# Thirty-two experts on one core: the turns of the gated rows and of the next rows move into the middle of the weight products

## The reference, cut to what matters

```
a = xb @ w_gate[e]                       # 1024 x 512
b = xb @ w_up[e]                         # 1024 x 512
y = (silu(a) * b) @ w_down[e]            # 512 x 1024
```

## Time and profile before

| | us |
|---|---|
| median of 3 runs | 2085.39 (2083.49 to 2088.24) |
| the profiled execution, its own time | 2085.79 |
| its span in the profile | 2084.0 |
| TensorE busy | 1966.2 (94% of the span) |
| VectorE busy | 1188.4 (57%) |
| ScalarE busy | 970.2 (47%) |
| 32 experts, from the first GM to the last | 292.2 to 877.9 in the span |

### The profile page before, as it was taken

One profiled execution on the slowest core, in us unless ns is written; L12 is line 12 of the kernel. 1 busy time (PEld: TensorE's weight loads), 2 busy tenths in 40 slices (PEclk: granted clock), 3 DMA queues, 4 the chain that ended last, 5 costly groups with the idle time before them and its releaser, 6 DMA issues.

```text
span 2084.0 us, 22887 instructions
## 1 busy us (share of the span) xinstructions
PE 1966.2 (94%) x8924; PEld 1572.5 (75%) x8924; DVE 1188.4 (57%) x1547; ACT 970.2 (47%) x1469; POOL 186.4 (9%) x250
## 2 busy tenths in 40 slices
PE   4989989999999999989999999998999989999997
PEld 3758767777777777758888888886777768888886
DVE  7776688888888888862543333324345343333322
ACT  3433268778878787744232222124445442222221
POOL 3100110121211110010000000001011100000000
PEclk8999999999999999999999999999999999999999
DMA  8464479999999999952323323222112123323211
GB/s 282 158 210 168 172 245 337 352 352 368 357 351 349 345 335 349 331 174 81 101 81 101 102 81 101 91 91 84 61 41 81 41 68 125 101 98 101 87 39 41
DMA packets 199832, 366.49 MB, mean 176 GB/s; under 512 B 13450, under 2 KB 83863, under 8 KB 199722
## 3 DMA queue, kind: packets, MB, share of 16 engines
q1 hardware_dynamic: 180960, 342.91, 47.6%
q10 hardware_dynamic: 8714, 11.46, 1.6%
q0 software_dynamic: 10048, 10.62, 1.5%
HBM read 365.05 MB, written 24.65 MB: 187 GB/s over the span
## 4 chain that ended last, share of the span: by engine, by line
PE 87%; DVE 7%; DMA 2%; issue 2%; ACT 1%; SPq 1%; POOL 0%; DVEq 0%; POOLq 0%; ACTq 0%
PE ps L263 85%; DVE wlo L210 2%; DMA raw<-in_w_in 1%; PE ps L2031 1%; DVE GM L2104 1%; SPq L886 1%; PE ps L731 1%; DMA raw<-in_ada_w 0%; DMA raw<-in_w_expert_down 0%; DVE acc L260 0%; PE ps L2608 0%; DVE hT5l L260 0%; DVE hT4l L769 0%; DVE X L845 0%; ACT XN L689 0%
## 5 line engine op out<-in xcount | busy, mean ns | idle before, releaser
L210 DVE TENSOR_TENSOR wlo<-raw,whi 128x1024 fp32r<-128x1024 f32 (+1 forms) x576 | 671.5, 1216 | 317.2 <-ACT whi L191 313.7
L191 ACT ACTIVATE whi<-raw 128x1024 fp32r<-128x1024 f32 (+1 forms) x576 | 573.0, 1047 | 232.8 <-PE ps L263 215.2
L263 PE MATMUL ps<-hT5h,whi 128*128 128x512 f32 x352 | 137.8, 391 | 6.3 <-DVE wlo L210 6.3
L263 PE MATMUL ps<-hT5l,whi 128*128 128x512 f32 x352 | 137.5, 391 | 0.0
L263 PE MATMUL ps<-hT3h,whi 128*128 128x512 f32 x352 | 137.0, 389 | 0.6 <-DVE hT3l L260 0.6
L263 PE MATMUL ps<-hT5h,wlo 128*128 128x512 f32 x352 | 137.4, 390 | 0.0
L263 PE MATMUL ps<-hT3l,whi 128*128 128x512 f32 x352 | 136.9, 389 | 0.0
L263 PE MATMUL ps<-hT3h,wlo 128*128 128x512 f32 x352 | 136.9, 389 | 0.0
L2471 DVE TENSOR_TENSOR tmpT<-tmpT,ps 128x512 f32<-128x512 f32 x44 | 30.1, 684 | 139.6 <-PE ps L263 139.6
L263 PE MATMUL ps<-whi,XT1h 128*128 128x512 f32 x256 | 102.1, 399 | 0.0
L263 PE MATMUL ps<-whi,XT0h 128*128 128x512 f32 x256 | 101.0, 395 | 1.1 <-DVE XT0l L2057 1.1
(11 more groups left out here) (446 smaller groups left out, 4062.5 us busy)
## 6 DMA issues: line engine op xcount, KB each, us to landing
raw<-in_w_expert_gate SPq DMA_DIRECT2D x64, 1024.0 KB, 8.2
raw<-in_w_expert_up SPq DMA_DIRECT2D x64, 1024.0 KB, 8.0
raw<-in_w_expert_down SPq DMA_DIRECT2D x64, 1024.0 KB, 6.7
raw<-in_ffn_w_gu SPq DMA_DIRECT2D x44, 1024.0 KB, 5.0
raw<-in_ffn_w_down SPq DMA_DIRECT2D x20, 1024.0 KB, 5.0
raw<-in_ada_w SPq DMA_DIRECT2D x24, 512.0 KB, 5.4
raw<-in_w_in SPq DMA_DIRECT2D x8, 1024.0 KB, 5.7
raw<-in_a_w_in SPq DMA_DIRECT2D x8, 1024.0 KB, 9.3
```

The source lines that it names most:

```text
L191: e.activation(hi[:, c], raw[:, c], ACT.Copy).then_inc(self.S("w_hi"), 1)
L210: e.tensor_tensor(lo[:, c], raw[:, c], hi[:, c].bitcast(F32), ALU.subtract).then_inc(self.S("w_lo"), 1)
L263: return e.matmul(o, l, r, start=start, stop=stop, skip_group_check=True)
```

## The change

The arithmetic is the same. Only the order on three engines and the plan of banks change. The product routine gets a call between its two halves (12 matmuls each). In it `eg` of n runs the 4 transposes of the gated rows of n-1, and `eu` of n runs the 8 transposes of the rows of n+1. ScalarE's and VectorE's loops put the copies of these between the items of the two halves, so that the items that belong to a product's first and second half are taken one at a time (`take_act(e, name, i)`). The last expert's gated rows are turned after its `eu`, as before.

```
@@ the plan of banks
         for n in range(NE):
+            if n > 0:
+                R.plan(f"et{n - 1}", 1, V_)
             R.plan(f"eg{n}", 1, A_)
...
+            if n + 1 < NE:
+                R.plan(f"x{n + 1}", 2, V_)
             R.plan(f"eu{n}", 1, V_)
...
-            if n + 1 < NE:
-                R.plan(f"x{n + 1}", 2, V_)
-            R.plan(f"et{n}", 1, V_)
+        R.plan(f"et{NE - 1}", 1, V_)
         R.plan(f"ey{NE - 1}", 2, A_)
@@ TensorE
-        def rows_in_pe(e, n, name):
+        def rows_in_pe(e, n, name, between=None):
...
                 if q == 0:
                     i.then_inc(S("w_used"), 1)
+                    if between is not None:
+                        between()
...
+        def turn_gated_pe(e, n):
+            b = R.claim(e, f"et{n}")
+            if n == NE - 1:
+                idle_pe(e, b, 2)
+            e.wait_ge(*R.done(f"eu{n}"))
+            for k in range(4):
+                i = e.transpose(b[:, k * P:(k + 1) * P], GM[:, k * P:(k + 1) * P], ident[:, :])
+            i.then_inc(*R.fill(f"et{n}"))
...
             for n in range(NE):
-                rows_in_pe(e, n, "eg")
+                rows_in_pe(e, n, "eg", (lambda: turn_gated_pe(e, n - 1)) if n > 0 else None)
                 if n > 0:
                     rows_out_pe(e, n - 1)
-                rows_in_pe(e, n, "eu")
-                if n + 1 < NE:
-                    turn_pe(e, n + 1)
-                b = R.claim(e, f"et{n}")
-                if n == NE - 1:
-                    idle_pe(e, b, 2)
-                e.wait_ge(*R.done(f"eu{n}"))
-                for k in range(4):
-                    i = e.transpose(b[:, k * P:(k + 1) * P], GM[:, k * P:(k + 1) * P], ident[:, :])
-                i.then_inc(*R.fill(f"et{n}"))
+                rows_in_pe(e, n, "eu", (lambda: turn_pe(e, n + 1)) if n + 1 < NE else None)
+            turn_gated_pe(e, NE - 1)
             rows_out_pe(e, NE - 1)
@@ ScalarE
+            def gated(n):
+                if n > 0:
+                    e.wait_ge(*R.full(f"ey{n - 1}", 1))
+                e.wait_ge(*R.full(f"et{n}"))
+                e.activation(GTs[0][:, :, :], R.bank(f"et{n}")[:, :].rearrange("p (c n) -> p c n", c=4),
+                             ACT.Copy).then_inc(S("gt_hi"), 1)
             for n in range(NE):
-                take_act(e, f"eg{n}")
+                take_act(e, f"eg{n}", 0)
+                if n > 0:
+                    gated(n - 1)
+                take_act(e, f"eg{n}", 1)
...
-                take_act(e, f"eu{n}")
+                take_act(e, f"eu{n}", 0)
                 if n + 1 < NE:
                     turn_act(e, n + 1)
-                if n > 0:
-                    e.wait_ge(*R.full(f"ey{n - 1}", 1))
-                e.wait_ge(*R.full(f"et{n}"))
-                e.activation(GTs[0][:, :, :], R.bank(f"et{n}")[:, :].rearrange("p (c n) -> p c n", c=4),
-                             ACT.Copy).then_inc(S("gt_hi"), 1)
+                take_act(e, f"eu{n}", 1)
+            gated(NE - 1)
@@ VectorE
+            def gated(n):
+                e.wait_ge(S("gt_hi"), n + 1)
+                e.tensor_tensor(GTs[1][:, :, :], R.bank(f"et{n}")[:, :].rearrange("p (c n) -> p c n", c=4),
+                                GTs[0][:, :, :].bitcast(F32), ALU.subtract).then_inc(*R.free(f"et{n}"))
             for n in range(NE):
-                take_vec(e, f"eg{n}")
+                take_vec(e, f"eg{n}", 0)
+                if n > 0:
+                    gated(n - 1)
+                take_vec(e, f"eg{n}", 1)
                 if n > 0:
                     take_vec(e, f"ed{n - 1}")
-                take_vec(e, f"eu{n}")
+                take_vec(e, f"eu{n}", 0)
+                if n + 1 < NE:
+                    turn_vec(e, n + 1)
+                take_vec(e, f"eu{n}", 1)
                 e.wait_ge(*R.done(f"eg{n}"))
...
                 e.tensor_tensor(GM[:, :], SG[n % 2][:, :], R.bank(f"eu{n}")[:, :], ALU.mult).then_inc(*R.free(f"eu{n}"))
-                if n + 1 < NE:
-                    turn_vec(e, n + 1)
...
-                e.wait_ge(S("gt_hi"), n + 1)
-                e.tensor_tensor(GTs[1][:, :, :], R.bank(f"et{n}")[:, :].rearrange("p (c n) -> p c n", c=4),
-                                GTs[0][:, :, :].bitcast(F32), ALU.subtract).then_inc(*R.free(f"et{n}"))
+            gated(NE - 1)
```

More of the change, by code:

```diff
@@ L2019, in experts_pe, with take_act, take_vec @@
             for n in range(NE):
-                rows_in_pe(e, n, "eg")
+                rows_in_pe(e, n, "eg", (lambda: turn_gated_pe(e, n - 1)) if n > 0 else None)
                 if n > 0:
                     rows_out_pe(e, n - 1)
-                rows_in_pe(e, n, "eu")
-                if n + 1 < NE:
-                    turn_pe(e, n + 1)
-                b = R.claim(e, f"et{n}")
-                if n == NE - 1:
-                    idle_pe(e, b, 2)
-                e.wait_ge(*R.done(f"eu{n}"))
-                for k in range(4):
-                    i = e.transpose(b[:, k * P:(k + 1) * P], GM[:, k * P:(k + 1) * P], ident[:, :])
-                i.then_inc(*R.fill(f"et{n}"))
+                rows_in_pe(e, n, "eu", (lambda: turn_pe(e, n + 1)) if n + 1 < NE else None)
+            turn_gated_pe(e, NE - 1)
             rows_out_pe(e, NE - 1)
         AHEAD = W.index["gv"][2]
-        def take_act(e, name):
-            for j in W.index[name]:
+        def take_act(e, name, i=None):
+            for j in W.index[name] if i is None else [W.index[name][i]]:
                 W.high(e, min(j + W.depth(j), AHEAD))
-        def take_vec(e, name):
-            for j in W.index[name]:
+        def take_vec(e, name, i=None):
+            for j in W.index[name] if i is None else [W.index[name][i]]:
                 W.low(e, min(j + W.depth(j), AHEAD))
```

## The result

| | before, us | after, us |
|---|---|---|
| median of 4 runs | 2086.52 (2083.49 to 2088.24) | 2052.10 (2044.28 to 2052.41) |
| span of the profiled execution | 2084.0 | 2050.4 |
| first GM to last GM | 292.2 to 877.9 | 293.7 to 844.3 |
| a quiet expert, GM to GM | 18.79 | 17.72 |

The ratio after to before is 0.9827, 95% interval 0.9807 to 0.9847: 1.7% faster. The forecast was 2055 us, with steps of 17.7 to 17.9.

The account below looks back on a forecast made before the run. TensorE and VectorE in series bound it, TensorE idling while GM is made; 13 x 1.00 + 17 x 1.09 + 2.5 = 34.0 us, less 3 for late loads, saves 31: 2055 us, range 2047 to 2068.

Parts of the forecast that it names:

- The idle time removed: TensorE's idle time between products goes at 31 boundaries: 1.09 us per expert, step 18.79 to 17.70 us.
- the forecast's two workings: Two estimates of twelve transposes' time, 1.2 and 1.31 us, leaving 1.15 or 1.04 us of the 2.35 us gap idle.
- The two waits inside products: TensorE's new waits for GM in the middle of eg and for GTl at ed; both were to be covered.
- The covers: Time to spare before TensorE needs GM in mid-eg, 0.4 us, and GTl at ed, 0.5 us.
- the walk: Stepping through ScalarE's and VectorE's queues with profiled durations: GM ends at 2.3 us, GTl at 5.3, a step is 17.7.
- The first boundary: Between the first two experts, half of eg runs in TensorE's 4 us idle gap: 2.5 us gained.
- The loads: Weight loads from HBM limit the gain: 375 GB/s in the first 13 experts, and 3 us off for late loads.
- the rate: Needed 377 GB/s in the first stretch, 375 taken: first 13 experts at 17.79 us, the other 17 at 17.70.
- Rival A: Loads bound the kernel: 2063 us if 362 GB/s is the ceiling, 2073 us if 355; chance 0.21.
- Its sign: What would show A: ScalarE's whi waiting for loads for tens of us.
- Rival B: VectorE becomes the bound, waiting behind ScalarE at XTl and GTl: steps of 19.2 us, 2097 us; chance 0.03.
- Rival C: The gap returns inside the product, GM as late as before: 2085 us, 0.7 us brackets before GM's transposes; chance 0.04.

Follow-up runs that it names:

- The two halves alone: Two runs against the kernel before: only the gated rows turned inside eg, 2098.46 us; only the next rows turned inside eu, 2133.99 us.
- the doubled GM: Changed kernel with the whole of GM done once more on VectorE, into a scratch tile, ahead of GM: 2058.43 us, ratio 0.9861.
- GTl twice: Changed kernel with GTl's work done once more on VectorE, into a scratch tile, ahead of GTl: 2054.65 us, ratio 0.9853.
- the copies directly behind GM: Changed kernel with the gated rows' copies GTh (ScalarE) and GTl (VectorE) put directly behind GM, ahead of the weight items: 2069.56 us, ratio 0.9936.

## Why the prediction was right

**The idle time removed.** Forecast 1.09 us per expert, steps of 17.70. Measured 1.07 and 17.72. The 0.02 is less than the 0.1 by which the forecast's two workings (1.04 and 1.15) differ. The first matmul after transposes has its successor 0.32 us behind it instead of 0.23, and that now happens twice per expert; whether this is the 0.02 no run shows.

**The two waits inside products** cost nothing in quiet experts, as walked. The covers are 0.46 and 0.63 us, a little thicker than the 0.4 and 0.5 of the walk. The two halves alone and the doubled GM bear out the walk by steps given beforehand (about 19.2, 19.5 to 20.0, 17.9 to 18.0 against 19.27, 19.97, 17.86). Two steps were missed: GTl twice came out at 17.75 where 17.8 to 17.9 was walked, and the copies directly behind GM at 17.95 to 19.7 where it was 18.7 to 18.9, summed on ScalarE while VectorE set the shortest steps.

**The first boundary.** Forecast 2.5 us. The first step is 3.76 shorter and its start 1.5 later: 2.26.

**The loads** are the term that was mis-sized. I took off 1.2 us for a rate of 375 GB/s in 13 experts and 3 us for late loads, 4.2 together. Between the first step and the last, the profiled execution lies 2.1 us over 29 steps of 17.72; the two more profiles of the same kernel lie 3.4 and 4.9 over. The kernel before had 0.8 of its own of that kind. So 1.3 us more was lost than before in the profile that the result rests on, and 2.6 and 4.0 in the others: the 4.2 was too much for two of three and near for the third, whose last step, 16.3 us, made up for some of it. The last step gave back 0.5 us that the sum did not have. 2.9 and 0.5 gained on the forecast, less 0.6 for thirty steps of 0.02 and 0.25 at the first boundary, is about the 2.6 us between 2054.8 and the profiled execution's 2052.2.

Of the two parts of that term, the rate was none: 378 GB/s was reached without a pause once the loads were no longer late. That the changed kernel shows 375 GB/s in its first stretch, the figure that the forecast took for a ceiling, is luck: it is what steps of about 17.8 us carry.

**Rival A** (loads bind at 355 to 362 GB/s) is refuted by the same window. Its sign was a poor one: ScalarE's waits for expert loads between 300 and 850 us are 18.8, 27.5 and 28.1 us in the three profiles, nearly the "tens of us" that were to show A, and came from late loads. The figure that the prediction took from the Trainium skill, "DMA: Bandwidth & Descriptors", section Specifications, is about 358 GB/s for one core. As a limit for this core the traces do not agree with it: 375 and 378 over 250 us. The same page of the Trainium skill says, in its section Bandwidth, that each core gets about 358 when both cores that share the memory stream; this kernel ran on one core, and no run here has a second. **Rival B** needed 18.8 us of VectorE per expert; it has 229.95 in 250 us, 16.3 per step. **Rival C** would have shown brackets before the transposes of GM in every expert; there are seven, and 11 and 10 in the other two profiles.

## What to carry to other kernels

When an engine idles because a product, a copy and a transpose follow each other, count the whole chain of both things that could fill the gap before moving one of them: here each move alone made the kernel slower, since one had been the cover of the other. Work put inside a product must come with the order of the queues that feed it, and an in-order queue that waits for it holds up everything behind. Here a DMA share of 1.00 was no bound: look for the engine that waits for loads, and if there is one, see whether the loads leave late or are split too late before believing that the engines are full. A step is not an engine's work plus its wait: an engine that waits may only have room to spare, so follow the loop that closes on itself.

## What the runs showed of the hardware that I had not expected

The DMA share read 1.00 at 355 GB/s and 1.02 at 378 GB/s, and taking out 1 of the 6 MB of an expert in the kernel before changed nothing beyond 3 us, so the share in these windows does not tell how much is left.

The granted clock fell in about every third expert of the kernel with only the next rows moved, though the pauses ahead of the transposes of GM were 2.08 us where it fell and where it did not; each fall added 1.6 us to a step. In the kernel before, with pauses of about 1.1 us per expert, it read 1.00 from 300 to 850 us.
